# Two-layer streaming encoder on 8 cores: all block conversion in the first layer, from slot one on; the second tile's x behind one block and its norm's sum in PSUM; v first at the layer's turn

## What is computed

```python
h = rmsnorm(x, norm_g)
proj = h @ w_in              # a_b a_c a_x a_z | b_in b_z | c_u c_v c_z | g_a g_b g_c
y_a = a_b * causal_dwconv(a_c * a_x, 3 taps) * silu(a_z)
glu = b_in[..., :W] * sigmoid(b_in[..., W:])
y_b = silu(layernorm(causal_dwconv(glu, 31 taps) + bias)) * silu(b_z)
v   = layernorm(gelu(c_v))
y_c = gelu(c_u) * chunk_spatial_mix(v, w_s, b_s) * silu(c_z)
m = sum over branches k: sigmoid(g_k + gb_k) * (y_k @ w_branch_k)
x = x + m @ w_out
```

## Time and profile before

| | |
|---|---|
| runs, us | 4062.06, 4698.89, 4042.81 (median 4062.06) |
| the profiled execution's own time, us | 4045.41 |
| its span (slowest core), us | 4043.5 |
| spans of the 8 cores, us | 4025.3 to 4043.5 |
| PE busy | 3906.7 us, 97% |
| DVE busy | 3377.1 us, 84% |
| POOL busy | 2809.1 us, 69% |
| ACT busy | 2708.3 us, 67% |
| DMA queue q1 (SP) | 697.11 MB, 52.2% of 16 engines |
| DMA queue q0 (POOL) | 113.25 MB, 18.2% of 16 engines |
| wring<-wall | 517 loads of 1024 KB, median 6.2 us to landing |
| wring<-wblk | 83 loads of 1024 KB, 12.6 us |
| wall<-wring | 43 stores of 1024 KB, 11.1 us |
| wall<-wblk | 50 halves of 512 KB, 8.4 us |

### The profile page before, as it was taken

The page is one execution under the profiler, slowest core; times in us unless marked ns, Lnnn a source line. Parts: engine busy times, 40 slices in busy tenths (PEclk is TensorE's granted clock), DMA queues, the critical chain, the costliest instruction groups (busy, mean ns, idle before and its releaser), DMA issues.

```text
span 4043.5 us, 76617 instructions; the slowest of 8 cores (4025.3 to 4043.5 us)
## 1 busy us (share of the span) xinstructions
PE 3906.7 (97%) x19936; PEld 1956.3 (48%) x20174; DVE 3377.1 (84%) x5639; ACT 2708.3 (67%) x4510; POOL 2809.1 (69%) x2925
## 2 busy tenths in 40 slices
PE   6999999999999999999999999999999999999997
PEld 2444444444444565655444444444444455555553
DVE  6988678898879788888887888889898888888884
ACT  5766667767556577777766667666676757677763
POOL 4868588794948384968686785849577475868680
PEclk8999999999999999999999999999999999999999
DMA  7979795865988787777888889554554557666653
GB/s 167 198 157 203 178 225 192 189 208 174 231 213 221 223 249 222 232 228 232 214 216 214 185 196 225 177 187 177 183 178 167 204 174 246 212 233 212 205 201 123
DMA packets 168237, 815.89 MB, mean 202 GB/s; under 512 B 19584, under 2 KB 47104, under 8 KB 85504
## 3 DMA queue, kind: packets, MB, share of 16 engines
q1 hardware_dynamic: 148224, 697.11, 52.2%
q0 software_dynamic: 19152, 113.25, 18.2%
q10 hardware_dynamic: 432, 0.61, 0.1%
HBM read 841.57 MB, written 106.69 MB: 235 GB/s over the span
## 4 chain that ended last, share of the span: by engine, by line
PE 84%; DMA 5%; issue 4%; DVE 4%; ACT 3%; POOL 1%; SPq 0%; DVEq 0%; another core or an unknown queue 0%; ACTq 0%; POOLq 0%
PE ps L486 78%; PE ps L1013 4%; DMA wring<-wblk 2%; DVE ps L297 1%; DMA wring<-wall 1%; DVE co L293 1%; ACT tmp_t L285 1%; PE ps L1167 1%; ACT ps L285 1%; DMA wall<-wring 1%; POOL pacc L293 0%; ACT L285 0%; DVE tmp_t L293 0%; ACT co L285 0%; DMA ya<-mT 0%
## 5 line engine op out<-in xcount | busy, mean ns | idle before, releaser
L486 PE MATMUL ps<-hT,wring 128*128 128x512 bf16 (+2 forms) x13644 | 2776.8, 360 | 65.7 <-ACT tmp_t L285 13.9
L293 POOL TENSOR_TENSOR pacc<-pacc,prod 128x512 f32<-128x512 f32 (+2 forms) x1550 | 1786.8, 1181 | 390.5 <-ACT prod L285 387.4
L486 PEld LDWEIGHTS ps<-hT,wring 128*128 128x128 bf16 x13808 | 1348.4, 98 | 1398.5 <-issue 92.1
L297 DVE SCALAR_TENSOR_TENSOR ps<-gluT,par_t,ps 128x512 f32<-128x512 bf16 (+2 forms) x2626 | 1678.1, 699 | 26.2 <-ACT ps L285 25.9
L285 ACT ACTIVATE prod<-gluT,par_t 128x512 f32<-128x512 bf16 (+2 forms) x1586 | 1036.5, 678 | 300.2 <-POOL pacc L293 296.2
L285 ACT ACTIVATE tmp_t<-ps 128x512 f32<-128x512 f32 (+2 forms) x738 | 403.4, 554 | 408.0 <-PE ps L486 379.0
L293 POOL TENSOR_TENSOR tmp_t<-tmp_t 128x512 f32<-128x512 f32 (+2 forms) x288 | 331.7, 1157 | 164.7 <-DVE tmp_t L297 110.9
L297 DVE SCALAR_TENSOR_TENSOR tmp_t<-tmp_t,ps 128x512 f32<-128x512 f32 (+2 forms) x432 | 273.5, 633 | 195.3 <-PE ps L486 151.0
L285 ACT ACTIVATE tmp_t<-ps,par_t 128x512 f32<-128x512 f32 (+2 forms) x432 | 275.4, 641 | 240.1 <-PE ps L486 232.4
L486 PE MATMUL ps<-ya,wring 128*128 128x512 bf16 (+2 forms) x1139 | 248.1, 360 | 5.0 <-DVE hT L297 3.8
L486 PE MATMUL ps<-yb,wring 128*128 128x512 bf16 (+2 forms) x1140 | 248.3, 359 | 1.0 <-DVE yb L293 0.3
(11 more groups left out here) (94 smaller groups left out, 3161.1 us busy)
## 6 DMA issues: line engine op xcount, KB each, us to landing
wring<-wall SPq DMA_DIRECT2D x517, 1024.0 KB, 6.2
wring<-wblk POOLq DMA_DIRECT2D x83, 1024.0 KB, 12.6
wall<-wring SPq DMA_DIRECT2D x43, 1024.0 KB, 11.1
wall<-wblk POOLq DMA_DIRECT2D x50, 512.0 KB, 8.4
xr<-xin SPq DMA_DIRECT2D x48, 256.0 KB, 15.4
x<-xr SPq DMA_DIRECT2D x40, 256.0 KB, 10.4
xn<-x SPq DMA_DIRECT2D x40, 256.0 KB, 8.2
xr<-x SPq DMA_DIRECT2D x40, 256.0 KB, 6.7
```

The costliest lines, as they stand in the source:

```text
L293: S.op(eng, lambda e: e.tensor_tensor(out=out, in0=in0, in1=in1, op=op), reads=reads, writes=writes, cost=ecost(eng, out, False))
L297: S.op("dve", lambda e: e.scalar_tensor_tensor(out=out, in0=in0, scalar=scalar, in1=in1, op0=op0, op1=op1), reads=reads, writes=writes, co ...
L486: ins = e.matmul(B(b, NT), lhsT=wtile(s, t, kk), rhs=rhs(kk), start=(kk == 0), stop=(kk == 7))
```

## The change

- `conv_l1` is started right after B1 of item 0. It first converts up to `AHEAD` = 8 blocks of layer 0 (M1, M4, M7, M10, B2-1, M5, M11, O1) as long as item 1's M phase hasn't begun; seven of them come to be converted, and are then loaded from `wall` by all. After layer 0 is complete it converts all 34 blocks of layer 1 in the order of use. `CROOM` goes from -1 to 0: the model clock of the DMA engines may reach that of TensorE.
- `rms_stats` on VectorE keeps the sum of squares in a PSUM bank instead of a `tmp_t` buffer.
- In the start only block 0 is issued ahead of the x loads of item 1, and these wait for block 0 instead of block 1; then `ring_pump` issues the others.
- Item 9 runs V before B1, as item 3 does; `conv_finish` of item 8 is moved from the end of slot 8 to between V and B1 of slot 9.
- A store's model latency goes from 2 to 6 (`lat`); that is only an estimate of the scheduler.

By count of instructions: wring<-wblk 83 to 50, wall<-wblk 50 to 82, wall<-wring 43 to 27, wring<-wall 517 to 550. Lines behind a helper move by one (L285, L293, L297, L315, L486 are L286, L294, L298, L316, L487 after), L1013 is L1022.

```diff
--- before.py
+++ after.py
@@ -19,12 +19,13 @@
 NTMP = 10
 NPROD = 4
 NBLK = 34
+AHEAD = 8
 TPREP = 1
 B2AT = 6
 VAT = 2
 PATF = (0,)
 PATL = (2, 1, 3)
-CROOM = -1.0
+CROOM = 0.0
 R_CBB, R_LBG, R_LBB, R_CA, R_NG, R_FG = 0, 1, 2, 3, 6, 7
 R_HALF = 8
 R_GB, R_LCG, R_CB = 8, 11, 12
...
@@ -107,7 +108,7 @@
         self.free[eng] = start + cost
         if is_dma:
             self.pipe = max(self.pipe, start + cost) + pipe
-            self.fin[(tok[0], tok[1])] = self.pipe + 2.0
+            self.fin[(tok[0], tok[1])] = self.pipe + lat
         else:
             self.fin[(tok[0], tok[1])] = start + cost + (0.2 if eng == "pe" else 0.1)
         waits = []
...
@@ -450,7 +451,7 @@
             l, b = plan[n][1], blk_id(plan[n][2])
             if n in raw and ("wall", l, b) not in S.last_w and use_no[n] >= store_no[b]:
                 DMA(wall[l, b], wring[:, n % NSLOT, :], (("w", n % NSLOT),), (("wall", l, b),), "ws%d" % (n % NSLOT),
-                    pipe=3.03)
+                    pipe=3.03, lat=6.0)
 
         def store_pump():
             for n in range(max(ring["use"], NSLOT), ring["next"]):
@@ -530,26 +531,34 @@
             NT = it["NT"]
             if ok is not None:
                 yield lambda: ok(0)
-            acc = tmps.get()
+            if eng == "dve":
+                yield lambda: len(banks.q) >= 3
+                ab = banks.get()
+                acc, ra = B(ab, NT), PB(ab)
+            else:
+                at = tmps.get()
+                acc, ra = tmp_t[:, at, 0:NT], TM(at)
             for c in range(8):
                 if ok is not None:
                     yield lambda c=c: ok(c)
                 yield ("act", ((xname, c),), ())
                 if c == 0:
-                    ACT(tmp_t[:, acc, 0:NT], xt[:, c, 0:NT], AF.Square, ((xname, c),), TM(acc))
+                    ACT(acc, xt[:, c, 0:NT], AF.Square, ((xname, c),), ra)
                 else:
                     t = tmps.get()
                     ACT(tmp_t[:, t, 0:NT], xt[:, c, 0:NT], AF.Square, ((xname, c),), TM(t))
                     yield (eng, TM(t), ())
-                    TT(tmp_t[:, acc, 0:NT], tmp_t[:, acc, 0:NT], tmp_t[:, t, 0:NT], ALU.add, TM(acc) + TM(t), TM(acc),
-                       eng=eng)
+                    TT(acc, acc, tmp_t[:, t, 0:NT], ALU.add, ra + TM(t), ra, eng=eng)
                     tmps.put(t)
-            yield ("act", TM(acc), ())
+            yield ("act", ra, ())
             yield free_lock
             lock[0] = True
-            for y in hi_lo(tmp_t[:, acc, 0:NT], TM(acc), NT, 0, eng):
+            for y in hi_lo(acc, ra, NT, 0, eng):
                 yield y
-            tmps.put(acc)
+            if eng == "dve":
+                banks.put(ab)
+            else:
+                tmps.put(at)
             yield ("pe", (("hl", 0, 1),), ())
             yield lambda: len(banks.q) >= 3
             b = banks.get()
@@ -1403,7 +1412,7 @@
                     addp(pv, *b2)
                 addp(pv, *[("M", q) for q in range(2, 12, 3)])
             else:
-                addp(it, *(vv + first if n == 3 else first + vv))
+                addp(it, *(vv + first if n in (3, nt_all) else first + vv))
                 if pv is not None:
                     addp(pv, ("B2", 0), ("B2", 1), *[("M", q) for q in range(12)])
             addp(it, *(pa if n == 0 else []), ("UZ", 0))
@@ -1431,10 +1440,12 @@
         g0 = norm(items[0], "dve", lambda: True, lambda: True)
         for _ in range(9):
             next(g0)
-        ring_pump()
-        cn1 = Chain(norm(items[1], "dve", lambda: True, lambda: True, None, (xb, "xr"), ("w", 1)), "norm1")
+        emit_load(0)
+        ring["next"] = 1
+        cn1 = Chain(norm(items[1], "dve", lambda: True, lambda: True, None, (xb, "xr"), ("w", 0)), "norm1")
         for _ in range(8):
             cn1.step()
+        ring_pump()
         hv = par[:, :, :, R_HALF:NROW].rearrange("p l c r -> p (l c) r")
         TS(hv, hv, 0.5, ALU.mult, ("par",), ("par",))
         for _ in g0:
@@ -1447,30 +1458,32 @@
                 tick()
 
         def conv_l1():
+            ahead = [("M", 1), ("M", 4), ("M", 7), ("M", 10), ("B2", 1), ("M", 5), ("M", 11), ("O", 1), ("M", 8), ("M", 2),
+                     ("O", 0)]
             used = [("B1", 4), ("V", 2), ("UZ", 4), ("A", 8), ("B2", 2), ("M", 12), ("O", 2)]
             order = [W_PHASE[k] + q for k, m in used for q in range(m)]
             t = now[0]
             cvn = 0
-            yield lambda: all(("wall", 0, b) in S.last_w for b in range(NBLK))
-            for b in order[1::2] + order[::2]:
+            jobs = [(0, W_PHASE[k] + q) for k, q in ahead[:AHEAD]] + [(1, b) for b in order]
+            for l, b in jobs:
+                if l:
+                    yield lambda: all(("wall", 0, b) in S.last_w for b in range(NBLK))
                 yield lambda: now[0] > t and S.pipe <= S.free["pe"] + CROOM
-                if ("wall", 1, b) in S.last_w:
+                if ("wall", l, b) in S.last_w or (l == 0 and items[1]["m_on"]):
                     continue
                 for hf in range(2):
                     t = now[0]
                     hs = slice(hf * 2048, hf * 2048 + 2048)
-                    DMA(wall[1, b][:, hs], wblk[1, b][:, hs], (), (("wall" if hf else "wh", 1, b),), "cv%d" % (cvn % 8),
+                    DMA(wall[l, b][:, hs], wblk[l, b][:, hs], (), (("wall" if hf else "wh", l, b),), "cv%d" % (cvn % 8),
                         eng="pool", pipe=3.6)
                     cvn += 1
                     if not hf:
-                        yield lambda: now[0] > t and S.pipe <= S.free["pe"] + CROOM
+                        yield lambda: now[0] > t and (l == 0 or S.pipe <= S.free["pe"] + CROOM)
 
         for n, it in enumerate(items):
             pv = items[n - 1] if n else None
             it["pv"] = pv
             nx = items[n + 1] if n + 1 < len(items) else None
-            if n == 3:
-                Chain(conv_l1(), "cv")
             cn = None
             if nx is not None:
                 mac1 = n in (1, 2)
@@ -1484,6 +1497,7 @@
             if n == 0:
                 later(TPREP, lambda: c0.append(Chain(prep_ws(0), "ws0")))
                 drive(ph_B1two(it, nx, cn))
+                Chain(conv_l1(), "cv")
                 sw = Chain(b1_swap(nx, it), "swap")
                 prep_go[0] = True
                 drive(ph_V(it))
@@ -1510,7 +1524,7 @@
                 else:
                     conv_finish(pv)
                     drive(ph_B1(it, pv))
-            elif n == 3:
+            elif n in (3, nt_all):
                 drive(ph_V(it))
                 conv_finish(pv)
                 drive(ph_B1(it, pv))
@@ -1554,7 +1568,7 @@
                 cp = Chain(prep_ws(1), "ws1")
             if n > 1:
                 drive(ph_A(it))
-            if nx is not None and n > 2:
+            if nx is not None and n > 2 and n + 1 != nt_all:
                 conv_finish(it)
             for c in cf:
                 c.finish()
```

6 lines of the change are left out of this document (3 added, 3 removed).

## The result

Over 18 runs each, the changed kernel takes 1.0094 times as long as the one before (95% interval 1.0063 to 1.0126): some 38 us slower, where 4025 us and a gain of 20 were forecast. The median of all its 18 runs is 4103.86 us (4065.54 before), its profiled execution took 4097.78. On another chip, with both kernels measured again, the ratio was 1.0061 (1.0044 to 1.0079), 25 us.

What follows compares the result with a forecast made beforehand. TensorE, busy 3906.7 of 4043.5 us, was taken as the bound. Terms 6 - 8.9 - 1.6 + 2 - 6.8 + 5 - 17.6 + 1.5 = -20.4 took 4045.4 to 4025.0 us, likeliest range 4008 to 4040.

Steps and rivals of the forecast that it cites:

- Start: Kernel start: x loads go out earlier, but squares ahead of the first tanh delay item 1's hT; +6 us.
- rival B: Kernel start: the second tile's x comes at once, so the start gains 4 us; 4015 us, chance 0.10.
- Ahead conversion: Slots 0 to 2: 379 wait goes, -8.9 us; three smaller raw-block waits go, -1.6; halves delay a raw block, +2.
- rival D: Slots 1 and 2: raw loads wait behind halves, waits at 379 and 1032 stay or move; 4047 us, chance 0.18.
- 1032: TensorE's 4.47 us wait on an M block at 1032.29 us goes, with its half-clock time; -6.8 us.
- Dense conversion: Layer 1's conversion between about 1089 and 2013 us: most blocks in time, some late at joins; +5 us.
- Rival A: 384-column tiles: DMA congestion, blocks taking over 16 us to land throughout, TensorE follows DMA; 4079 us, chance 0.13.
- Layer 1's raw loads: Layer 1: no raw blocks, so waits at 2124, 2157, 2300 and 2529 us go; -17.6 us.
- the turn: Item 9, V first: the 1954 us wait goes, but one on `co` as in slot 3 is expected; +1.5 us.
- Rival C: Layer's turn: no stall, because V's matmuls cover the 15 adds; 4016 us, chance 0.09.

Runs made afterwards that it cites:

- e2: Changed kernel with AHEAD = 0, so no layer 0 block is converted ahead; ratio to the kernel before 1.0058.
- e5: Kernel before with the dense conversion alone (CROOM = 0.0, layer 1 blocks in order of use); ratio to the kernel before 1.0031.
- e9: Kernel before, blocks in order of use, no wait for all of layer 0, CROOM 0 up to slot 5, then -1; ratio 1.0039.
- e17b: Kernel before with CROOM = -0.3 and blocks in order of use; die 0 of chip E took 4030.6 us in the mean, before 4033.4.
- e18_best: e17b with the norm's sum in PSUM besides; die 0 of chip E took 4022.0 us in the mean, the kernel before 4033.4.
- e16: Kernel before with CROOM = 1.0, no hold, blocks in order of use; die 0 of chip E took 4099.2 us in the mean, before 4033.4.
- c_after2: The changed kernel run again on chip E; die 0 took 4055.8 us in the mean, the kernel before 4033.4.

## Why the prediction was wrong

Two steps failed: the term for the dense conversion (+5, measured +22 to +28) and the net gain of the blocks converted ahead (-8.5, measured +9 to +14 in slots 0 to 2). Both put the cost of background transfers on foreground ones near nothing. Step by step, in the forecast's own order; measured values are means of the cores from the table.

- **Start, +6.** Right in mechanism and size: hT of item 1 at 75.23 where 75.5 was worked out; squares of x ahead of the first tanh (43.8 for 43.5, though the forecast's own terms, 41 + 0.6 + 1.3, give 42.9). In the slots it is worth only about 3. The PSUM bank's share was put at 3.9 and measured 3.2. The rule cited from the Trainium skill (DMA: Bandwidth & Descriptors, "Queues, rings and completion order"), read as a whole chunk passing in one turn, would have had x land at once; here the first chunk landed 13.2 us after its issue, the median 23.1. So rival B is out.
- **Ahead conversion, -8.9 - 1.6 + 2.** This step failed, with the wrong sign: +9 to +14 in slots 0 to 2. The step counted a wait that goes (379, gone indeed on core 0) and halves ahead of raw blocks on one queue, bounded at +8, and left out every other transfer that the halves slow down: gluT<-yb at the end of slot 0 (11.9 us to land), raw blocks in slot 1 (6.67 us at 312). And the raw M blocks of slot 2, which it did price, were late by 5.3 to 7.0 us on four cores. It was also read on core 0: that core waited 7.7 us for raw blocks in slots 0 to 2, the mean of the cores 4.6, so there was less to gain. This is rival D's sign, new waits on raw M blocks in slot 2, and rival D had these slots right: by its prices they lose 12.4 us, start included, where 12.7 and 17.0 were measured. The wait at 1032, which D kept, went.
- **1032, -6.8.** The wait went: -7.3 on core 0, which is what was read, but 3.3 in the mean of the cores. It is AHEAD's doing (e2 +3.0, e5 -0.4), so this term belongs to the one above.
- **Dense conversion, +5 (bounds 0 and +20).** This is the other step that failed: +22 to +28 in the mean of the cores, outside its own bounds. The window at 2400 (95% busy, TensorE 99.5%) was taken as proof that 95% costs nothing; it holds 15 loads per 100 us, and the dense stretch asks for 17 to 18 at that share. And a usual landing was set against a mean lead of 16 us. Usual landings were even shorter than the 13.7 assumed (10.5 to 11.1), but 7 to 10% of the blocks took over 16, against 0.2% before, and the losses follow that share. That TensorE waits for just those blocks, most of all where the lead is short, as at V1, is argued; no wait was matched to its block. Rival A had the mechanism and twice the size (59); its own sign, more than 16 us throughout, did not come.
- **Layer 1's raw loads, -17.6, and the turn, +1.5.** Together -16.1 forecast, -16.1 measured in the first profile, -14.8 on chip C, the turn's wait included (6.08 for 7.1). The mechanism is right; that the first number agrees to the tenth is luck, since the terms were read on core 0, and there the gain was 20.5 and 19.6. Rival C is out.
- **The sum.** The table's first row adds up to +16 for the mean core and its second to +27, against a ratio of 25 us on that chip; forecast was -20. Of the difference of 47 on chip C, 23 are the dense conversion and 25 the conversion ahead with the term for 1032 (+10.0 where -15.3 was forecast); the start is 2.5 better and the raw loads 1.3 worse. On core 0, for which the forecast was made, the first profile has +8.5, -7.3, +17.6 and -20.5 against its own slots before, the second +22.6, -7.2, +25.4 and -19.6: in the first its span comes out 2 us shorter, in the second the four groups add up to 21 longer, so one core in one execution says little. The 31 us of the 0.81 stretch in the first profile come on top; no step thought of a clock below full that doesn't follow a wait.

## What to carry to other kernels

Background transfers can be nearly free up to a point and dear soon behind it: here 35 halves in four slots cost 1 to 9 us, 41 cost 12, 52 cost 22 to 28, 56 cost 78. e9's 26 halves would look cheap by this list and cost 15, with 17 of them in one slot, so the pace, and not the count, is what to set. The busiest window with no loss is only evidence for windows with the same demand. To price such transfers, don't set the median landing against the mean lead; look at how many loads take longer than the lead. And where a transfer is added, look at what else is in flight, the small copies with an engine waiting behind them first of all; the price is theirs. Terms that are waits on DMA should be read on all cores: the slowest core was slowest by having more of them.

## What the runs showed of the hardware

The granted clock can stand at 0.81 for 15 to 163 us on two neighbouring cores at once; in the 163 us, TensorE was busy without a break (162.98 us). This is not one of the stretches at 0.50 that stand beside TensorE's waits (3.4 to 20.6 us). It came in no profile from chips B, C and D, the changed kernel's own among them. On chip E it came in the changed kernel's profile and in those of e17b, e18_best and e16, and c_after2's die 1 had 122 to 139 such stretches, 755 to 858 us in all, on each of its cores.

Beside 52 conversion halves in 800 us, the slow tail of the block loads grew more than the median: from 6.3 to 10.5 us in the median on core 0, and from 0.2% to 7.2% of the loads over 16 us.
